# A two-block transformer pass on one Trainium2 core: bank-by-bank order for two groups of matmuls, and squares by halves in the norm between them

## What is computed

```python
        x = x + m @ w_out[l]                        # output projection
        h = rmsnorm(x, norm2_g[l])                  # norm "ffn"
        ...
        x = x + (jax.nn.gelu(u_gate) * u_val) @ ffn_down[l]   # down product, 2816 rows of weights
    return rmsnorm(x, final_g)                      # joined with the next norm: "m0"
# second block, first layer
        rmsnorm_2(h, norm_mix[l])
```

## Time and profile before

| What | Value |
|---|---|
| Time, median of 3 runs | 1840.06 us (1838.62 to 1841.4) |
| The profiled execution, its own time | 1842.44 us |
| Its span, first to last instruction | 1840.3 us |
| PE busy, share of the span | 1552.2 us, 84% |
| DVE, ACT, POOL busy | 761.5, 598.3, 77.7 us |
| Mean granted clock of PE | 0.924 of full speed |
| Read from HBM | 563.73 MB, 307 GB/s over the span |
| Output projection, second column half, ends | about 304 us into the span |
| Down product ends | about 497 us |
| First expert's matmuls begin | about 742 us |

### The profile page before, as it was taken

One profiled execution on the slowest core, in us unless ns is written; L12 is line 12 of the kernel. 1 busy time (PEld: TensorE's weight loads), 2 busy tenths in 40 slices (PEclk: granted clock), 3 DMA queues, 4 the chain that ended last, 5 costly groups with the idle time before them and its releaser, 6 DMA issues.

```text
span 1840.3 us, 34072 instructions
## 1 busy us (share of the span) xinstructions
PE 1552.2 (84%) x15322; PEld 1188.2 (65%) x15322; DVE 761.5 (41%) x1530; ACT 598.3 (33%) x1061; POOL 77.7 (4%) x89
## 2 busy tenths in 40 slices
PE   8999999999999999976666656899998875676665
PEld 7989998999899998533333323799896432333332
DVE  6796668887465666210100110546664110111011
ACT  5765646665455654000000000546642000000001
POOL 2020001000020101000000000001010000000000
PEclk9999999999999999987887898999999978878887
DMA  7443456545473558999999999844488999999997
GB/s 279 167 163 138 146 187 229 190 183 201 159 276 118 204 230 359 388 430 429 431 431 428 431 429 429 358 177 145 185 350 342 430 429 431 429 431 429 429 430 299
DMA packets 46000, 568.02 MB, mean 309 GB/s; under 512 B 6752, under 2 KB 7296, under 8 KB 10656
## 3 DMA queue, kind: packets, MB, share of 16 engines
q1 hardware_dynamic: 40032, 552.62, 73.4%
q0 software_dynamic: 3952, 12.55, 2.0%
q10 hardware_dynamic: 1872, 0.69, 0.1%
HBM read 563.73 MB, written 2.10 MB: 307 GB/s over the span
## 4 chain that ended last, share of the span: by engine, by line
PE 63%; DMA 32%; another core or an unknown queue 2%; DVE 2%; ACT 1%; issue 0%; SPq 0%; ACTq 0%; DVEq 0%
DMA slab<-in_slabs 32%; PE bank L566 14%; PE bank L567 14%; PE bank L568 14%; PE bank L1083 6%; PE bank L1126 3%; PE bank L540 2%; PE bank L1139 1%; PE bank L909 1%; PE bank L968 1%; PE bank L1060 1%; PE bank L932 1%; PE bank L578 0%; PE bank L586 0%; PE bank L582 0%
## 5 line engine op out<-in xcount | busy, mean ns | idle before, releaser
L1083 PE MATMUL bank<-slab,xe 128*32 128x256 f32 x4096 | 318.4, 468 | 155.4 <-DMA slab<-in_slabs 154.1
L1161 DVE TENSOR_TENSOR wl<-slab,wh 128x1024 fp32r<-128x1024 f32 (+1 forms) x286 | 348.1, 1231 | 192.2 <-ACT wh L1782 191.9
L566 PE MATMUL bank<-hth,wh 128*128 128x256 f32 x1344 | 387.6, 288 | 0.1
L567 PE MATMUL bank<-htl,wh 128*128 128x256 f32 x1344 | 380.0, 283 | 0.0
L568 PE MATMUL bank<-hth,wl 128*128 128x256 f32 x1344 | 379.9, 283 | 0.0
L1782 ACT ACTIVATE wh<-slab 128x1024 fp32r<-128x1024 f32 (+1 forms) x286 | 296.3, 1047 | 158.6 <-PE bank L568 158.5
L1083 PEld LDWEIGHTS bank<-slab,xe 128*32 128x32 f32 x4096 | 144.7, 129 | 310.9 <-DMA slab<-in_slabs 197.5
L566 PEld LDWEIGHTS bank<-hth,wh 128*128 128x128 f32 x1344 | 257.2, 191 | 12.8 <-issue 10.5
L567 PEld LDWEIGHTS bank<-htl,wh 128*128 128x128 f32 x1344 | 257.5, 192 | 0.1
L568 PEld LDWEIGHTS bank<-hth,wl 128*128 128x128 f32 x1344 | 257.3, 191 | 0.0
L1126 PE MATMUL bank<-slab,ha 128*32 128x256 f32 x2048 | 143.5, 430 | 76.4 <-DMA slab<-in_slabs 73.5
(11 more groups left out here) (369 smaller groups left out, 2186.4 us busy)
## 6 DMA issues: line engine op xcount, KB each, us to landing
slab<-in_slabs SPq DMA_DIRECT2D x251, 2048.0 KB, 47.9
slab<-in_slabs SPq DMA_DIRECT2D x23, 1024.0 KB, 10.7
bias<-in_bias POOLq DMA_DIRECT2D x32, 192.0 KB, 3.3
bias<-in_bias POOLq DMA_DIRECT2D x8, 256.0 KB, 6.1
x<-in_x SPq DMA_DIRECT2D x2, 512.0 KB, 4.4
rg<-in_rg POOLq DMA_DIRECT2D x1, 1024.0 KB, 8.9
scratch<-rel POOLq DMA_DIRECT2D x4, 256.0 KB, 5.2
out<-x SPq DMA_DIRECT2D x2, 512.0 KB, 2.6
```

The source lines that it names most:

```text
L566: e.matmul(o, wh, xh, start=start, stop=False, skip_group_check=True)
L567: e.matmul(o, wh, xl, start=False, stop=False, skip_group_check=True)
L1083: t = e.matmul(bk[bank][32 * j:32 * j + 32, 0:256], XE[:, c, :], w[:, k, 256 * j:256 * j + 256], start=(c == 0), stop=(c == 7))
L1161: e.tensor_tensor(lo, src, hi.bitcast(F32), ALU.subtract).then_inc(*dve_l.mark(p))
```

## The change

Three things are edited; nothing is computed otherwise than before, up to the order of additions.

1. `project_blocks`: for the first block's second column half, pieces j = 2 and 3 are multiplied row block by row block (row block 0 with both pieces, then row block 1 with both) in place of piece by piece. `pe_w` of piece j is marked in row block 1.
2. The down product's last two pieces (20 and 21) are multiplied bank by bank.
3. The joint norm's squares and weighted squares go by halves for both row blocks. DVE's weighted squares and small sums of row block 0 are put between the adds of the banks. The weighted square of half 0 starts from 1e-12 and the small sums chain it with q, so that the second half's small sum gives the bias of the root; the sum of the two q halves, for the second root, comes last. In `norm("m0")` PE's keep is given two steps in place of three, and the keep after the reciprocals is left out for `m0`.

```diff
+    Q0, Q1, W0, B0 = (c_mx[:, 2 * i:2 * i + 2] for i in range(4))
...
             if tag == "m0":
-                keep([(act_s, ("sq0", tag)), (dve_s, ("s2", tag, 0)), (dve_s, ("s2", tag, 1))], 4, 3)
+                keep([(act_s, ("sq", tag, 0, 1)), (dve_s, ("s2", tag, 1, 0))], 4, 3)
             else:
                 keep([(act_s, ("sq0", tag)), (dve_s, ("sq1", tag))], 4, 3)
-            keep([(dve_s, ("rs", tag, 0)), (dve_s, ("rs", tag, 1))], 2, 3)
+                keep([(dve_s, ("rs", tag, 0)), (dve_s, ("rs", tag, 1))], 2, 3)
...
+        def project_blocks(M, p):
+
+            for tb in range(2):
+                q = slice(tb * 128, (tb + 1) * 128)
+                for j in (2, 3):
+                    wh, wl = halves(p + 4 + j, 2, 512)
+                    P.wait_ge(*merged_low("f", j))
+                    for k in range(2):
+                        kk = 2 * j + k
+                        t = mm3(bk[6 + tb][:, :], M.h[:, kk, q], M.l[:, kk, q], wh[:, k, :], wl[:, k, :],
+                                start=False, stop=(kk == 7))
+                    if tb:
+                        t.then_inc(*pe_w.mark(p + 4 + j))
+                if tb == 0:
+                    t.then_inc(*pe_s.mark(("po", "f", 1)))
+                reader[6 + tb] = [(dve_s, ("po", "f", 1, tb))]
...
                 for j in range(4):
+                    if l == "f" and i == 1 and j == 2:
+                        return project_blocks(M, p)
...
+        for kk in range(20):
+            for b in range(4, 8):
+                if kk == 0:
+                    bank_free(b)
+                t = down(kk, b)
+            t.then_inc(*pe_w.mark(first["down", 0] + kk))
+        for b in range(4, 8):
+            t = down(20, b)
+            if b == 7:
+                t.then_inc(*pe_w.mark(first["down", 0] + 20))
+            t = down(21, b)
+            if b < 7:
+                t.then_inc(*pe_s.mark(("acc", "f", b)))
+        t.then_inc(*pe_w.mark(first["down", 0] + 21))
...
+        def weighted_square(tb, h):
+            s, (to, init) = slice(512 * h, 512 * h + 512), ((W0, 1e-12), (c_ss[:, 4:6], 0.0))[h]
+            e.tensor_tensor_reduce(out=XSQ[:, tb, s], in0=XSQ[:, tb, s], in1=FG2[:, s], scale=1.0, scalar=init, op0=ALU.mult,
+                                   op1=ALU.add, accum_out=to[:, tb:tb + 1]).then_inc(*dve_s.mark(("s2", "m0", tb, h)))
+
+        def small_sum(tb, h):
+
+            to, q, w = ((B0, Q0, W0), (c_ss[:, 6:8], Q1, B0))[h]
+            V.wait_ge(*dve_s.now)
+            e.scalar_tensor_tensor(to[:, tb:tb + 1], q[:, tb:tb + 1], 1e-6, w[:, tb:tb + 1], ALU.mult,
+                                   ALU.add).then_inc(*dve_s.mark(("sb", tb, h)))
+
+        def first_weighted(b):
+            if b == 4:
+                V.wait_ge(*pool_s["fg2"])
+            elif b < 7:
+                V.wait_ge(*act_s["sq", "m0", 0, b - 5])
+                weighted_square(0, b - 5)
+                small_sum(0, b - 5)
+        add_banks("f", pe_w[N1 - 1], first_weighted)
+        V.wait_ge(*dve_s["ab", "f", 3])
+        V.wait_ge(*act_s["sq", "m0", 1, 0])
+        weighted_square(1, 0)
+        small_sum(1, 0)
+        V.wait_ge(*act_s["sq", "m0", 1, 1])
+        weighted_square(1, 1)
+        small_sum(1, 1)
+        V.wait_ge(*dve_s["sb", 0, 1])
+        e.tensor_tensor(c_ss[:, 0:2], Q0, Q1, ALU.add).then_inc(*dve_s.mark("s1"))
...
+            for h in range(2):
+                A.wait_ge(*dve_s["ab", "f", 2 * tb + h])
+                s = slice(512 * h, 512 * h + 512)
+                square(XSQ[:, tb, s], X[:, tb, s], (Q0, Q1)[h][:, tb:tb + 1], ("sq", "m0", tb, h))
+        for tb in range(2):
+            A.wait_ge(*dve_s["sb", tb, 1])
             e.activation(c_rs[:, 2 + tb:3 + tb], c_ss[:, 4 + tb:5 + tb], ACT.Sqrt,
                          bias=c_ss[:, 6 + tb:7 + tb]).then_inc(*act_s.mark(("rt", "m0", tb)))
+        A.wait_ge(*dve_s["s1"])
         e.activation(c_rs[:, 0:2], c_ss[:, 0:2], ACT.Sqrt, bias=c_eps).then_inc(*act_s.mark("r1"))
```

More of the change, by code:

```diff
@@ L856, in tensor_program, with down @@
             reader[b] = [(dve_s, ("upc", n))]
-        for kk in range(22):
-            p = first["down", 0] + kk
-            wh, wl = halves(p, 1, 1024)
+        def down(kk, b):
+            tb, hf = (b - 4) // 2, b % 2
+            q, c = slice(tb * 128, (tb + 1) * 128), slice(hf * 512, (hf + 1) * 512)
+            wh, wl = halves(first["down", 0] + kk, 1, 1024)
             P.wait_ge(*dve_s["at", kk // 2])
[L861 to L872, removed]
+            return mm3(bk[b][:, :], AT.h[:, kk, q], AT.l[:, kk, q], wh[:, 0, c], wl[:, 0, c],
+                       start=(kk == 0), stop=(kk == 21))
+        for kk in range(20):
[12 more added lines that the diff above has]
+        t.then_inc(*pe_w.mark(first["down", 0] + 21))
         for b in range(4, 8):
@@ L1373, in project, with add_banks @@
                                            ALU.add).then_inc(*dve_s.mark(("po", l, i, tb)))
-        def add_banks(l, last):
+        def add_banks(l, last, then=None):
             for b in range(4, 8):
@@ L1380, in add_banks @@
                 e.tensor_tensor(xs, xs, bk[b][:, :], ALU.add).then_inc(*dve_s.mark(("ab", l, b - 4)))
+                if then is not None:
+                    then(b)
         def last_square(tag, out_):
@@ L2062, in scalar_program @@
         table(ACT.Sqrt)
[L2063 to L2068, removed]
-        for tb in range(2):
-            A.wait_ge(*dve_s["s2", "m0", tb])
-            A.wait_ge(*dve_s["s1", "m0"])
+        for tb in range(2):
+            for h in range(2):
[4 more added lines that the diff above has]
+            A.wait_ge(*dve_s["sb", tb, 1])
             e.activation(c_rs[:, 2 + tb:3 + tb], c_ss[:, 4 + tb:5 + tb], ACT.Sqrt,
                          bias=c_ss[:, 6 + tb:7 + tb]).then_inc(*act_s.mark(("rt", "m0", tb)))
+        A.wait_ge(*dve_s["s1"])
         e.activation(c_rs[:, 0:2], c_ss[:, 0:2], ACT.Sqrt, bias=c_eps).then_inc(*act_s.mark("r1"))
```

## The result

| | Before | After |
|---|---|---|
| Median of 20 runs, us | 1839.86 (1837.68 to 1842.93) | 1842.12 (1840.49 to 1845.91) |
| Profiled execution, us | 1842.44 | 1843.55 |
| Its span, us | 1840.3 | 1841.7 |
| Mean granted clock of PE | 0.924 | 0.928 |

The ratio is 1.0012, with a 95% interval of 1.0007 to 1.0018, so the change costs 1.3 to 3.3 us. The forecast was 1840.0 in a range of 1837.6 to 1843.0: the time lies in the range, the direction does not agree. The forecast put a loss of 1.36 and a gain of 1.44 against each other. In the trace both are there, and beside them 1.6 us that it gave to a rival with 14 in 100.

The account below looks back on a forecast made before the run. Up to the first expert PE's own order was taken to set the time. +1.36 for project_blocks and -1.44 for the joint norm gave -0.1 us, so 1840.0 us from the median of 1840.06; range 1837.6 to 1843.0.

Parts of the forecast that it names:

- rival with 14 in 100: Norm ffn: the wider gap ahead of the keep rows drops PE's clock to 0.50, costing 1.60 us; 14 in 100.
- What bounds the kernel: Up to the first expert PE's own order sets the time; microseconds won or lost before 690 us move later work one for one.
- project_blocks, +1.36: End of the output projection: piece 86 is released six matmuls later, delaying piece 89's parts and the keep rows by 1.36 us.
- The step that failed: The project_blocks cost bounded from above by 1.36 us, with a fall of the clock left out as a rival.
- The prediction's own sign of being wrong: Norm ffn's gap not growing, PEclk below 1.00 in either norm, or the first expert's start moving over 1 us.
- The first rival, bank 6 early, 1.04 won: End of the output projection: keep rows follow PE's end directly, 1.04 us won, 1837.6 us in total; 8 in 100.
- Down product bank by bank, 0: End of the down product: banks 4 to 6 are done earlier, and piece 152's release 2.04 us later costs nothing.
- The squares by halves and the keep rows, -1.44: Joint norm: ACT's root starts 0.48 us sooner and keep rows no longer hold the transposes 0.98; transposes 1.44 us sooner.
- The joint norm's clock: Joint norm: the clock stays up; a rival had it fall and stay low, net +3.3 us, 1843.3; 6 in 100.
- "Same" by the 0.2% bound: Whole kernel: time within 0.2%, 3.7 us, of before, given a chance of 0.86.

Follow-up runs that it names:

- blocks_only: The kernel before with the project_blocks edit alone; 1842.60 us, ratio 1.0018.
- both_norms_short: The adds_ahead kernel with norm ffn's piece 89 low part and POOL's product moved later and no keep behind the reciprocals; 1838.49 us, ratio 0.9986 against before.
- adds_ahead: The whole change with piece 89's high and low parts put behind ACT's square and DVE's adds of banks 6 and 7; 1839.64 us, ratio 0.9997 against before.
- down_banks_only: The kernel before with only the down product's last two pieces bank by bank; 1840.57 us, ratio 1.0000.
- norm_keep_back: The change without project_blocks, with the keep behind the joint norm's reciprocals put back; 1839.55 us, ratio 0.9996 against before.
- norm_only: The change without project_blocks; 1840.15 us, ratio 0.9999 against the kernel before.
- after_gap_filled: The whole change with eight identity matmuls that wait for nothing ahead of norm ffn's keep; 1841.04 us, ratio 1.0002 against the kernel before.
- after_again: The changed kernel, unedited, measured again; 1842.41 us, ratio 1.0009 against the kernel before.
- norm_only_again: A second set of runs of the change without project_blocks; 1839.24 us, ratio 0.9993 against the kernel before.
- keep_cut_only: The kernel before with only the joint norm's keep matmuls behind the reciprocals left out; 1839.17 us, ratio 0.9994.
- null_before: The kernel before, unchanged, measured against itself; 1840.14 us, ratio 0.9998.

## Why the prediction went wrong

- *What bounds the kernel.* The reading was right but for one detail: the transfers reach 430 GB/s from the eighteenth slice on, the two slices before show 359 and 388. In both places the chain runs as given, and what happens at 305 us reaches the end: blocks_only came out at +2.8 us in the mean for +3.0 in its trace. For the gain at 500 us this is less sure. Both_norms_short is faster beyond its interval, but its mean is -2.2 for -2.7 in the trace (see what stays open).
- *project_blocks, +1.36.* Right: the gap grew from 1.04 to 2.41 us. That the wait for piece 86 makes it is shown by adds_ahead.
- *The step that failed* is the bound from above of that term, "1.36 and a fall of the clock, treated as a rival", and the argument by which the rival got 14 in 100: "here PE was full with dense matmuls up to the gap". That fullness did not protect it. The clock fell in three of three traces, which made the keep rows 1.4 to 1.6 us dearer (1.57 in the first), and did not fall when the gap was filled. The rival's price of 1.60 was right; with it in the sum, the forecast would have been +1.5, which lies inside the measured interval. The prediction's own sign of being wrong, a PEclk below 1.00 in one of the two norms, came true.
- *The first rival, bank 6 early, 1.04 won.* It asked for another order on DVE, and adds_ahead gave it that: the keep rows follow PE's last matmul, yet the first matmul came no sooner. Only with the three further edits of both_norms_short 1.3 us are won.
- *Down product bank by bank, 0.* Right by itself (down_banks_only).
- *The squares by halves and the keep rows, -1.44.* The size is right (7.57 to 6.13 us). The split of it was less so: I gave 0.48 to the squares and 0.98 to the keep rows. ACT's root of row block 1 started 2.63 us behind PE's end (500.94), where the forecast had 2.89 and before was 3.37; so it came 0.74 sooner. And the whole 1.4 is there with the keep behind the reciprocals put back (norm_keep_back), so cutting that keep is no part of the gain beside the sooner squares. The small sums let the next instruction start before they end (497.02 and 497.10), so bank 7 was late by 0.2, not 0.4. The transposes take 1.97 us from their own start, in the timeline of before 1.91 (501.88 to 503.79); the 1.75 of the earlier trace rows counts from the end of the keep rows.
- *The joint norm's clock.* It stayed at 1.00, as forecast; its gaps were 0.77 and 0.96 us.
- *Chances.* "Same" by the 0.2% bound was right. That the time lies in the range is no merit of the sum: the range was wide enough for it, and the sum itself is 2.1 us too low. The forecast's direction hung on 0.1 us, less than the runs can tell; the fall of the clock decided it.

The Trainium skill's page Perfetto Trace Analysis says in the section "Optimizing Scalar/DVE Operations" that where the element-wise engines are not full but leave gaps on others, breaking instructions up may let the work be done sooner. The traces of the joint norm agree: 1.44 us, and as much in norm_keep_back.

What stays open: the kernels with the norm's edits came out somewhat slower in the mean than their traces say (the change +2.6 for +1.5, norm_only pooled -0.8 for -1.4, norm_keep_back -0.9 for -1.4, adds_ahead -0.8 for -1.4, after_gap_filled +0.7 for -0.1, both_norms_short -2.2 for -2.7; after_again, +1.4 for +1.4, and norm_only_again, -1.3 for -1.4, fit). Of the kernels without them keep_cut_only lies on the other side, -1.2 for -0.7. Each single difference is within what its runs allow, and some share their runs of before. The traces leave the same doubt. From the first matmul of the layer at 500 us to the end of the span, the five kernels without the norm's edits took 1334.0 to 1336.1 us, mean 1334.9, the eight with them 1335.3 to 1338.5, mean 1336.4; 0.37 of the difference is the last norm (below), and the time outside the span is shorter by as much. So the rival of norm_only, that a part of the gain is taken back later, is not excluded, and no place for it was found.

Two places with a scatter of their own can be named. At the head of the second layer the 24 keep rows took 5.44 to 5.49 us in norm_only, norm_only_again, norm_keep_back and both_norms_short, and 4.5 to 4.6 in all others. In those four the clock was at 0.50 already ahead of the keep rows (both_norms_short: PEclk 0.67 in the window 1159 to 1160, and the rows start at 1160.90); in the others it was at 1.00 there and fell about as they started (before: 1.00 from 1160 to 1164, the rows start at 1165.14). But from the start of these rows to the end the four took no longer than the others, with the 0.37 taken off: 674.5 to 675.6 us against 673.7 to 676.4. So they do not explain the missing half microsecond. And from the first matmul of the layer to the first expert's, null_before, the same kernel, took 1.1 us less than the kernel before (237.25 and 238.35 us), with less time at the low clock ahead of the first expert (PEclk 0.92, 0.50, 0.72, 1.00 in the four windows of 738 to 746 us, before 0.61, 0.50, 0.50, 0.68). One trace can therefore not settle half a microsecond behind the joint norm.

## What to carry to other kernels

A new order of matmuls that finishes one bank sooner releases some other operand later: look up which engine waits for that release, and what else stands behind the wait in its own stream, before counting the early bank as a gain. If an edit widens an idle gap of PE, put the price of a fall of the clock into the sum itself as soon as the new gap comes near one in the same trace behind which the clock fell, whatever PE did before it. Idle matmuls in front of real ones cost as soon as what they wait for has become ready: check for each of them whether its operand's readiness or the filler is last.

## What the runs showed of the hardware that I had not expected

- With a gap of 2.41 us between dense matmuls and the keep rows the clock fell to 0.50 in three of three traces; with one of 1.04 or 1.05 us there it stayed at 1.00 in seven of seven, and so it did in the joint norm, with gaps up to 1.03 us, in all thirteen. The moment of the fall is not tied to the work: in the second trace of the change PEclk is 0.86 in the window 304 to 305, before the keep rows start at 305.13; in blocks_only, where they start at 305.41, it is still 1.00 from 305 to 306 and 0.60 from 306 to 307. The 24 rows took 4.37, 4.51 and 4.57 us.
- POOL's product of 1024 columns holds up DVE's scaling of 512 columns: two took 1.86 us beside it and 0.88 us without. It is the first of the two that pays, with 1.47 us in place of 0.48, and it ends 0.28 us behind the product (before: 307.88 and 307.60 us); the second takes 0.48 us again.
- In the last norm of the kernel, code that no edit touches, DVE's first reciprocal waits longer for ACT's root in kernels that have the norm's edits: 0.50 to 0.53 us in all eight, 0.15 or 0.16 in the five others. The row of before, and that of after:

```profile
1834.35 0.16 DVE L1174 RECIPROCAL sm<-sm 128x1 f32<-128x1 f32 x1 [0.15 <-ACT sm L1804]
```

```profile
1835.79 0.16 DVE L1201 RECIPROCAL sm<-sm 128x1 f32<-128x1 f32 x1 [0.53 <-ACT sm L1854]
```

That makes the span 0.37 us longer, while the time outside the span is shorter by about as much (2.1 us before, 1.8 after). Spans of kernels with different streams should not be compared to a few tenths.
